# The last expert unit written apart, and the tail after it worked by halves of 512 features

## The chip, the cores and the metric

The kernel runs on one core of one Trainium2 chip. The metric is the device time of one launch in microseconds (us); lower is better. A core has five engines with instruction queues of their own: TensorE (PE; its weight loads are shown apart as PEld), VectorE (DVE), ScalarE (ACT), GpSimd (POOL) and SyncE (SP). They meet only through semaphores. All data here is fp32.

## The reference, cut to what matters

One inference step of a hybrid network of two layers for 128 context tokens (`x_prompt`) and 128 latent tokens (`x_sample`), 256 tokens of 1024 features. The last sub-layer of the second layer is a mixture of experts with a gated, normalised residual. With `x` the residual stream, `h` its normalised and modulated copy, and `g_mod` the gate of that sub-layer:

```python
logits = h @ w_router                      # (256, 8)
top_v, top_i = lax.top_k(logits, 2)
top_w = softmax(top_v)
gate = sum(one_hot(top_i, 8) * top_w[..., None], axis=1)
out = 0
for e in range(8):                         # D_FF_EXPERT = 2816
    out = out + gate[:, e:e+1] * ((silu(h @ wg[e]) * (h @ wu[e])) @ wd[e])
x = x + g_mod * rms_norm(out, gain)        # rms over the 1024 features
```

`x` is then returned as `y_prompt` and `y_sample`.

## The kernel before, in words

Everything up to the routing is the same in both kernels. What matters is the expert stage, from about 860 us to the end.

**Units.** Tokens are not sent to experts one by one. For each expert the kernel builds a selection matrix `SEL` (token by place, 86 places, `CAP`), so that one product with it gathers the expert's tokens. A unit is one expert with up to 86 of its tokens. Each expert has one unit; an expert with more tokens has further ones, at most 13 in all (`UNITS`). How many there are is known only on the chip: VectorE writes it into the table `TBL` (`unit_count`, L2846, in the first unit after its hidden block 12). With the inputs timed here there are 8 units, 0 to 7.

**A unit.** The hidden width 2816 is cut into 22 blocks of 128 (`HB`). For each block `t` TensorE makes gate and up products from the gathered tokens `XG` (`gate_up`, L1466), ScalarE takes the SiLU (L1971), VectorE multiplies (`mixed`, L2860), and TensorE multiplies the result with a slice of the down weights into banks 4 and 5 (`down`, L1486). `down(t - 1)` stands behind `gate_up(t)` in TensorE's queue, so that the other two engines have a gate and up product's time. The weights (1 MB and 512 KB for each block) come through a ring of 11 slots, issued by SyncE in the order of use; SyncE waits until TensorE has used the slot (`tile_used`, L543).

**Between units.** Ahead of the last `down` of a unit TensorE gathers the tokens of the next one (`gather`, L1432, with the selection that VectorE made in `next_selection`), and ScalarE copies them to `XG` (L1986). The output of a unit is features by places. VectorE copies it out of the banks (`copy_y`, L2853), TensorE turns it (`turn_y`, L1442), ScalarE copies it to `YG`, TensorE scatters it back to tokens with the transposed selection `SELT` (`scatter`, L1448), and VectorE adds it, times the routing weight `GT1`, to the sum `O` (L2904). All that is done within the first blocks of the next unit.

**Loops.** The unit's code stands three times on TensorE, ScalarE and VectorE: unit 0; a loop over units 1 to 6; a loop from unit 7 to the unit count, which each engine reads into a register from `TBL` (L1532 and L1533, L1992 and L1993, L2916 and L2923). The last unit therefore gathers as well, for a next one that isn't there. SyncE has the same loops for the weights.

**After the last unit.** The tail has nothing beside it. TensorE signals `units_done` (L1535), VectorE copies both halves, TensorE turns all eight blocks and, once ScalarE has both halves of `YG`, scatters (four products into banks 0 to 3). VectorE makes the four additions (L2931), then signals ScalarE with a small copy (L2933). ScalarE squares `O` for each of the two token groups (`norm_o`, L1572), loads the table with the square root, and takes the root (L1582). Meanwhile VectorE multiplies `O` with the modulation gate `GB` into `TO` (`gated`, L2046); then it takes the reciprocal (L2012) and writes `X` (`residual`, L2065). GpSimd waits for both halves of `X`, issues the two stores (L607, L608) and waits for them. L195 is the end of the program, where each engine drains and all meet.

Of the kernel before, what the change touches and what calls it, by code (L numbers as in the profile page):

```python
# [24 lines left out]
ALU = mybir.AluOpType  # L25
# [3 lines left out]
P = 128  # L29
D = 1024  # L30
# [162 lines left out]
def program(nc, t, out):  # L193
    ctx = ExitStack()
    with ctx:  # L195
# [226 lines left out]

        class Counts:
# [16 lines left out]
            @contextmanager  # L440
            def in_loop(self, i, n, per):

                self.base, self.n, self.per, self.i = self.n, {}, per, i
                yield
                got, self.n, self.i = self.n, dict(self.base), None
                assert got == per, got
                for name, k in got.items():
                    self.n[name] = self.base.get(name, 0) + n * k

# [16 lines left out]
        def _(sp):  # L466
# [85 lines left out]
            with sp.Fori(NE - 1, sp.value_load(TBL[0:1, UNITS:UNITS + 1], min_val=NE, max_val=UNITS)) as u:  # L552
                expert_tiles(u, sp.value_load(TBL[0:1, bass.ds(u, 1)], min_val=0, max_val=NE - 1))


        @block.gpsimd
        def _(pool):
# [54 lines left out]
            pool.wait_ge(sem("stored_y"), 32)  # L612
# [3 lines left out]
        def _(pe):  # L616
# [839 lines left out]
            def unit(u):  # L1456
# [22 lines left out]
                def down(t, arrived, due, hid):  # L1479
# [9 lines left out]
                    taken(ins)  # L1489
# [18 lines left out]
                if later:  # L1508
                    pe.wait_ge(sem("unit_taken"), u * 4 - 2)
# [31 lines left out]
            scatter(1, 2, "last_scattered")  # L1541
# [3 lines left out]
        def _(act):  # L1545
# [416 lines left out]
            def unit(u):  # L1962
# [11 lines left out]
                for h in range(0 if isinstance(u, int) else 2):  # L1974
                    act.wait_ge(sem("y_turned"), u * 2 + (h - 1))
                    A(YG[0:CAP, h * 512:(h + 1) * 512], bank[6 + h][0:CAP, :], ACT.Copy).then_inc(sem("unit_yg"), 1)
# [3 lines left out]
                with act.Fori(0, LOOPS) as i:  # L1980
                    for t in range(2, 2 + ROWS):
                        silu(t, u * UT + i * (3 * ROWS) + (N_MOE + gate_taken(t)), u * HB + i * ROWS + (FT + t - 1))
                taken(u * UT + (N_MOE + up_taken(HB - 1)))
# [6 lines left out]
            with act.Fori(1, NE - 1) as u:  # L1990
                unit(u)
            act.wait_ge(sem("table"), 1)  # L1992
            with act.Fori(NE - 1, act.value_load(TBL[0:1, UNITS:UNITS + 1], min_val=NE, max_val=UNITS)) as u:  # L1993
                unit(u)
# [8 lines left out]
        def _(dve):  # L2003
# [57 lines left out]
            def residual(n):  # L2061
                rstd()
                dve.wait_ge(sem("gated"), 2 * (n + 1))
                for st in range(NST):
                    v.scalar_tensor_tensor(X[:, st, :], TO[:, st, :], SM[:, 6 + st:7 + st], X[:, st, :],  # L2065
                                           ALU.mult, ALU.add).then_inc(sem("x_final" if n == 3 else "x"), 1)
# [779 lines left out]
            def unit_count():  # L2846
                v.tensor_scalar(TBLF[:, UNITS:UNITS + 1], ORDER[:, 2 * NE - 1:2 * NE], float(NE), None, ALU.add).then_inc(made("dve_chain"), 1)
                dve.wait_ge(sem("dve_chain"), so_far("dve_chain"))
                v.tensor_copy(TBL[:, :], TBLF).then_inc(made("table"), 1)
# [45 lines left out]
            def unit(u):  # L2895
# [5 lines left out]
                for st, h in ((0, 0), (0, 1), (1, 0), (1, 1)):  # L2901
                    dve.wait_ge(sem("scattered"), u * 4 + (2 * st + h - 3))
# [7 lines left out]
                next_selection(u)  # L2910
# [5 lines left out]
            units = dve.value_load(TBL[0:1, UNITS:UNITS + 1], min_val=NE, max_val=UNITS)  # L2916
            for name, k in per.items():
                counts.n[name] = counts.n.get(name, 0) - k
            n0 = dict(counts.n)
            with dve.Fori(1, NE - 1) as u, in_loop(u, NE - 1, per):  # L2920
                unit(u)
            counts.n = n0
            with dve.Fori(NE - 1, units) as u, in_loop(u, NE, per):  # L2923
                unit(u)
# [64 lines left out]
```

## Time and profile before

| | us |
|---|---|
| median of 3 runs | 1580.46 |
| lowest, highest | 1577.77, 1585.19 |
| the profiled execution, its own time | 1576.2 |
| its span in the trace | 1574.3 |
| TensorE busy, of the span | 1487.2 (94%) |
| VectorE busy | 545.6 (35%) |
| ScalarE busy | 296.3 (19%) |
| mean granted clock of TensorE | 0.984 |

The span runs from the first to the last instruction of the profiled execution. An engine is busy while one of its instructions runs; what it waits for is inferred from semaphores. The clock is a share of TensorE's full 2.4 GHz.

### The profile page before, as it was taken

To read this page: it belongs to the slowest core of one execution; us is meant where nothing else is said; L and a number is where in the kernel's file an instruction comes from. 1 tells how busy PE (TensorE), PEld (TensorE's weight loads), DVE (VectorE), ACT (ScalarE), POOL (GpSimd) and SP (SyncE) were. 2 spreads that over 40 slices of the span, in tenths; PEclk is the share of its full clock that TensorE was granted. 3 is DMA by queue.
4 is the path that set the end of the run, shared out by engine and by line. 5 is a ranking of instruction groups with operands and counts; after the bars stand their busy time and mean duration, and the time that the engine had idled before them with its cause. 6 is when DMAs were issued, how large, how long until landed. Compare 5 with 4: busy or idle time off the path is not lost.

```text
span 1574.3 us, 62507 instructions
## 1 busy us (share of the span) xinstructions
PE 1487.2 (94%) x28005; PEld 1323.4 (84%) x28005; DVE 545.6 (35%) x1410; ACT 296.3 (19%) x817; POOL 16.4 (1%) x32
## 2 busy tenths in 40 slices
PE   5999888999998999999887999999999999999995
PEld 3888477999546787888866999999999999999995
DVE  1463435666636344666843301010101011010102
ACT  2112423010102432444324101010101010010101
POOL 0100000000000000000000000000000000000000
PEclk9999998999998999999998999999999999999998
DMA  9722676444448144000132799999999999999993
GB/s 391 292 82 100 250 300 270 161 174 181 182 167 314 40 162 150 6 8 8 33 151 81 300 417 379 416 386 418 384 412 409 387 419 380 418 376 417 376 418 131
DMA packets 72895, 407.07 MB, mean 259 GB/s; under 512 B 10514, under 2 KB 10948, under 8 KB 35908
## 3 DMA queue, kind: packets, MB, share of 16 engines
q1 hardware_dynamic: 68176, 398.92, 64.0%
q0 software_dynamic: 1184, 3.41, 0.7%
q10 hardware_dynamic: 3412, 2.93, 0.6%
q8 instruction: 98, 1.61, 0.4%
q14 instruction: 25, 0.20, 0.0%
HBM read 403.31 MB, written 1.92 MB: 257 GB/s over the span
## 4 chain that ended last, share of the span: by engine, by line
PE 37%; PEld 10%; DVE 1%; ACT 1%; issue 1%; PEldq 0%; DVEq 0%; POOL 0%; ACTq 0%
PE bank L1466 20%; PE bank L1486 10%; PEld bank L1466 7%; PEld bank L1486 3%; PE bank L644 2%; PE bank L1448 1%; PE bank L1432 1%; PE bank L1442 0%; PEld bank L1432 0%; PE bank L709 0%; PE bank L1267 0%; PEld bank L1448 0%; DVE w L2036 0%; DVE w L2675 0%; PE bank L1290 0%
## 5 line engine op out<-in xcount | busy, mean ns | idle before, releaser
L1466 PE MATMUL bank<-w,ring 128*64 128x86 f32 x11264 | 452.6, 237 | 1.1 <-ACT w L1959 0.6
L1466 PEld LDWEIGHTS bank<-w,ring 128*64 128x64 f32 x11264 | 432.4, 136 | 9.7 <-issue 8.8
L1486 PE MATMUL bank<-w,ring 128*64 128x86 f32 x5632 | 238.7, 237 | 0.0
L2860 DVE TENSOR_TENSOR w<-w,bank 128x86 f32<-128x86 f32 x176 | 43.1, 245 | 549.0 <-PE bank L1466 541.6
L1486 PEld LDWEIGHTS bank<-w,ring 128*64 128x64 f32 x5632 | 220.8, 137 | 0.0
L1971 ACT ACTIVATE w<-bank 128x86 f32<-128x86 f32 x176 | 42.8, 243 | 572.4 <-PE bank L1466 572.4
L641 PE MATMUL bank<-w,ring 128*128 128x256 f32 x256 | 59.1, 394 | 4.3 <-DVE w L2454 3.7
L641 PEld LDWEIGHTS bank<-w,ring 128*128 128x128 f32 x256 | 50.5, 198 | 13.0 <-DVE w L2454 4.0
L644 PE MATMUL bank<-ring,w 128*128 128x256 f32 x256 | 56.0, 380 | 1.9 <-DVE w L2036 1.9
L644 PEld LDWEIGHTS bank<-ring,w 128*128 128x128 f32 x256 | 48.4, 190 | 8.8 <-DVE w L2036 2.3
L667 PE MATMUL bank<-ring,ct 128*32 128x256 f32 x768 | 47.0, 396 | 2.4 <-ACT ct L1569 2.1
L1201 PE MATMUL bank<-ht 64*64 64x64 f32 x1280 | 45.6, 219 | 2.4 <-issue 1.6
L970 PE MATMUL bank<-w 128*128 128x128 f32 x352 | 44.4, 281 | 1.3 <-DVE w L2352 1.3
L970 PE MATMUL bank<-ht,ring 128*128 128x128 f32 x352 | 44.7, 282 | 0.6 <-DVE ht L2028 0.6
L1201 PEld LDWEIGHTS bank<-ht 64*64 64x64 f32 x1280 | 42.2, 135 | 3.2 <-issue 1.9
L970 PEld LDWEIGHTS bank<-w 128*128 128x128 f32 x352 | 42.5, 198 | 1.5 <-DVE ring L2316 1.5
L745 PE MATMUL bank<-ht,ring 128*128 128x256 f32 x192 | 43.5, 383 | 0.0
L970 PEld LDWEIGHTS bank<-ht,ring 128*128 128x128 f32 x352 | 42.7, 198 | 1.0 <-issue 1.0
L970 PE MATMUL bank<-w,ring 128*128 128x128 f32 x352 | 42.9, 275 | 0.0
L667 PEld LDWEIGHTS bank<-ring,ct 128*32 128x32 f32 x768 | 23.9, 114 | 22.1 <-issue 4.5
L1003 PE MATMUL bank<-ring,w 128*128 128x512 f32 x88 | 42.2, 592 | 0.0
L748 PE MATMUL bank<-ring,ht 128*128 128x256 f32 (+1 forms) x192 | 42.0, 372 | 0.0
(437 smaller groups left out, 1795.9 us busy)
## 6 DMA issues: line engine op xcount, KB each, us to landing
ring<-in_moe_gu SPq DMA_DIRECT2D x176, 1024.0 KB, 8.5
ring<-in_moe_w_down SPq DMA_DIRECT2D x176, 512.0 KB, 8.6
ring<-in_ada_w SPq DMA_DIRECT2D x48, 1024.0 KB, 5.0
ring<-in_ev_w_in SPq DMA_DIRECT2D x11, 1024.0 KB, 26.6
ring<-in_ffn_w_gate SPq DMA_DIRECT2D x11, 1024.0 KB, 7.9
ring<-in_ffn_w_up SPq DMA_DIRECT2D x11, 1024.0 KB, 5.2
ring<-in_ffn_w_down SPq DMA_DIRECT2D x11, 1024.0 KB, 6.4
ring<-in_ev_w_out SPq DMA_DIRECT2D x4, 1024.0 KB, 11.0
```

The lines of the kernel that those rows point to most:

```text
L641: ins = mm(b[:, a * TW:(a + 1) * TW], w[:, k, a * P:(a + 1) * P], src[:, k, :], start=k == 0, stop=k == KC - 1)
L644: ins = mm(b[:, a * TW:a * TW + n], src[:, k, a * P:(a + 1) * P], w[:, k, 0:n], start=k == 0, stop=k == KC - 1)
L667: ins = mm(sums_bank(n)[32 * q:32 * q + 32, 0:TW], CT[:, NST * k:NST * k + 32], w[:, k % 2, q * TW:(q + 1) * TW], start=k == 0, stop=k == ...
L745: ins = mm(b[:, a * TW:(a + 1) * TW], w[:, k, a * P:(a + 1) * P], HT[:, k, :], start=k == 0, stop=k == KC - 1)
L748: ins = mm(b[:, a * TW:a * TW + n], HT[:, k, a * P:(a + 1) * P], w[:, k, 0:n], start=k == 0, stop=k == KC - 1)
L970: ins = mm(region(j, r)[:, which * P:(which + 1) * P], lhs(which, k), rhs(k), start=first and which == 0 and k == 0, stop=k == 3, skip_gro ...
L1003: ins = mm(bank[DOWN_BANK[p]][:, :], lhs, rhs, start=n == 0, stop=n == FT - 1)
L1201: ins = mm(z_bank(lv, 0)[hp, (4 * d + j) * DH:(4 * d + j + 1) * DH], IZ[hp, d, j, :], IP[i % 2][hp, d, j, :], start=True, stop=True)
L1466: ins = [mm(b[hp, 0:CAP], w[:, k, hp], XG[:, k, :], start=k == 0, stop=k == KC - 1, skip_group_check=True) for hp in HALVES]
L1486: ins = [mm(bank[4 + c // 4][hp, (c % 4) * CAP:(c % 4 + 1) * CAP], w[:, c * P + hp.start:c * P + hp.stop], HIDU[:, t % 2, :], start=t == 0 ...
L1971: A(SILU[:, t % 2, :], bank[t % 2][:, 0:CAP], ACT.Silu).then_inc(sem("silu"), 1)
L2860: v.tensor_tensor(HIDU[:, t % 2, :], SILU[:, t % 2, :], bank[2 + t % 2][:, 0:CAP], ALU.mult).then_inc(sem("hid"), 1)
```

## The change

- The loop over units 1 to 6 now runs to a last unit that is read from the table, and that last unit is written apart, with its number `last` and the one before it, `prev`, in registers. TensorE, ScalarE and VectorE read both values behind unit 0 (VectorE writes two more entries of the table). With 8 units the loop still runs over 1 to 6 and unit 7 stands apart. SyncE's loops stay.
- The last unit has no gather, no copies to `XG` and no next selection. Its last `down` signals each half of its output on its own.
- The tail goes by halves of 512 features, `h`, and by token groups, `st`. Each half is copied, turned and copied to `YG` on its own; the scatter begins with half 0 for both groups. The piece `n = 2 h + st` is added, squared, gated and given its residual by itself. ScalarE loads the table with the square root ahead of the tail (`load_root`). The mean square is made in two steps: VectorE scales the first halves' sums and adds epsilon, and the root takes the second halves' sums with that as its bias.
- The stores are issued by SyncE, four of 256 KB (128 rows of 2 KB), each as its piece of `X` is written. GpSimd has none and waits for none.

```diff
 # SyncE
+            for n in range(4):
+                h, st = divmod(n, 2)
+                sp.wait_ge(sem("x"), 6 + n + 1)
+                sp.dma_start(out[("y_prompt", "y_sample")[st]][0][:, h * 512:(h + 1) * 512],
+                             X[:, st, h * 512:(h + 1) * 512]).then_inc(sem("stored_y"), 16)
+            sp.wait_ge(sem("stored_y"), 64)
 # GpSimd
-            pool.wait_ge(sem("x_final"), 2)
-            pool.dma_start(out["y_prompt"][0], X[:, 0, :]).then_inc(sem("stored_y"), 16)
-            pool.dma_start(out["y_sample"][0], X[:, 1, :]).then_inc(sem("stored_y"), 16)
...
-            pool.wait_ge(sem("stored_y"), 32)
 # TensorE
-            def unit(u):
+            def unit(u, prev=None):
...
+                        if prev is not None and t == HB - 1 and c % 4 == 3:
+                            ins[0].then_inc(sem("last_down"), 1)
+                            ins[1].then_inc(sem("last_down"), 1)
+                    if prev is None or t < HB - 1:
+                        taken(ins)
...
-                pe.wait_ge(sem("sel"), u + 2)
                 pe.wait_ge(sem("selt"), u + 1)
-                gather()
+                if prev is None:
+                    pe.wait_ge(sem("sel"), u + 2)
+                    gather()
                 down(HB - 1, "slot_last", u * 16 + 16, u * HB + (FT + HB))
...
-            with pe.Fori(1, NE - 1) as u:
+            pe.wait_ge(sem("table"), 1)
+            last = pe.value_load(TBL[0:1, UNITS + 1:UNITS + 2], min_val=NE - 1, max_val=UNITS - 1)
+            prev = pe.value_load(TBL[0:1, UNITS + 2:UNITS + 3], min_val=NE - 2, max_val=UNITS - 2)
+            with pe.Fori(1, last) as u:
                 unit(u)
-            pe.wait_ge(sem("table"), 1)
-            units = pe.value_load(TBL[0:1, UNITS:UNITS + 1], min_val=NE, max_val=UNITS)
-            with pe.Fori(NE - 1, units) as u:
-                unit(u)
-            pe.drain().then_inc(sem("units_done"), 1)
-            pe.wait_ge(sem("last_y"), 2)
-            pe.wait_ge(sem("xg"), units * 2 + 2)
-            turn_y("last_turned")
-            pe.wait_ge(sem("last_y"), 4)
-            scatter(0, 0, "last_scattered")
-            scatter(1, 2, "last_scattered")
+            unit(last, prev)
+            for h in range(2):
+                pe.wait_ge(sem("last_y"), h + 1)
+                for c in range(4 * h, 4 * h + 4):
+                    ins = tr(bank[6 + h][0:CAP, (c % 4) * P:(c % 4 + 1) * P], YT[:, c, :], ident)
+                ins.then_inc(sem("last_turned"), 1)
+            for h in range(2):
+                pe.wait_ge(sem("last_yg"), h + 1)
+                for st in range(NST):
+                    mm(bank[2 * st + h][:, :], SELT[:, st, :], YG[0:CAP, h * 512:(h + 1) * 512],
+                       start=True, stop=True).then_inc(sem("last_scattered"), 1)
 # ScalarE (its loops as on TensorE; unit(last, prev) ends ahead of the copies to XG)
+            load_root()
             for h in range(2):
                 act.wait_ge(sem("last_turned"), h + 1)
-                A(YG[0:CAP, h * 512:(h + 1) * 512], bank[6 + h][0:CAP, :], ACT.Copy).then_inc(sem("last_y"), 1)
-            act.wait_ge(sem("o_ready"), 1)
-            norm_o()
+                A(YG[0:CAP, h * 512:(h + 1) * 512], bank[6 + h][0:CAP, :], ACT.Copy).then_inc(sem("last_yg"), 1)
+            for n in range(4):
+                h, st = divmod(n, 2)
+                act.wait_ge(sem("o_ready"), n + 1)
+                A(W[9][:, n * 512:(n + 1) * 512], O[:, st, h * 512:(h + 1) * 512], ACT.Square,
+                  accum_out=SQ4[:, n:n + 1]).then_inc(sem("out_squares"), 1)
+            act.wait_ge(sem("meansq"), 4)
+            act.wait_ge(sem("out_squares"), 16 + 4)
+            for st in range(NST):
+                ins = A(SM[:, 4 + st:5 + st], SQ4[:, 2 + st:3 + st], ACT.Sqrt, scale=1.0 / D, bias=SM[:, 2 + st:3 + st])
+            ins.then_inc(sem("root"), 1)
 # VectorE (its loops as on TensorE; unit(last, prev) has no next_selection)
-            dve.wait_ge(sem("units_done"), 1)
-            copy_y("last_y")
-            for st in range(NST):
-                for h in range(2):
-                    dve.wait_ge(sem("last_scattered"), 2 * st + h + 1)
-                    o = O[:, st, h * 512:(h + 1) * 512]
-                    v.scalar_tensor_tensor(o, bank[2 * st + h][:, :], GT1[:, st:st + 1], o, ALU.mult, ALU.add).then_inc(made("dve_chain"), 1)
-                    dve.wait_ge(sem("dve_chain"), so_far("dve_chain"))
-            v.tensor_copy(SM[:, 199:200], SM[:, 6:7]).then_inc(sem("o_ready"), 1)
-            gated(3)
-            residual(3)
+            for n in range(2):
+                dve.wait_ge(sem("last_down"), 2 * n + 2)
+                v.tensor_copy(YT[:, 4 * n:4 * n + 4, :].rearrange("p c n -> p (c n)"),
+                              bank[4 + n][:, 0:4 * CAP]).then_inc(sem("last_y"), 1)
...
+            for n in range(4):
+                h, st = divmod(n, 2)
+                dve.wait_ge(sem("last_scattered"), n + 1)
+                v.scalar_tensor_tensor(piece(O, n), bank[2 * st + h][:, :], GT1[:, st:st + 1], piece(O, n),
+                                       ALU.mult, ALU.add).then_inc(sem("o_ready"), 1)
+            dve.wait_ge(sem("gb_copied"), 16)
+            for n in range(2):
+                dve.wait_ge(sem("o_ready"), n + 1)
+                v.tensor_tensor(piece(TO, n), piece(O, n), piece(GB, n), ALU.mult).then_inc(sem("gated"), 1)
+            dve.wait_ge(sem("out_squares"), 16 + 2)
+            v.tensor_scalar(SM[:, 2:4], SQ4[:, 0:2], 1.0 / D, EPS, ALU.mult, ALU.add).then_inc(sem("meansq"), 1)
+            for n in range(2, 4):
+                dve.wait_ge(sem("o_ready"), n + 1)
+                v.tensor_tensor(piece(TO, n), piece(O, n), piece(GB, n), ALU.mult).then_inc(sem("gated"), 1)
+            rstd()
+            for n in range(4):
+                st = n % 2
+                dve.wait_ge(sem("gated"), 6 + n + 1)
+                v.scalar_tensor_tensor(piece(X, n), piece(TO, n), SM[:, 6 + st:7 + st], piece(X, n),
+                                       ALU.mult, ALU.add).then_inc(sem("x"), 1)
```

Waits inside a unit that were written with `u * k + c`, `c` negative, are written for the last unit with `prev` instead (`shifted_by`), to the same value.

## Rows read from the trace of the kernel before

**Rows 1.** Windows: us, busy by engine, clock, DMA share, GB/s

```profile
...
890.00:1550.00 660.00, 659.31 (x16808) 638.79 (x16806) 80.38 (x270) 57.68 (x204) 0.00 (x0) 1.00 0.98 398
...
```

**Rows 2.** Waits of SyncE's queue, 870 to 1576 us: total, times, longest

```profile
...
SPq L544 <- PE bank L1466: 383.3, 148, 19.5
...
```

**Rows 3.** Timeline of the tail: start, us, engine, line, instruction [idle before]

```profile
...
1548.62 0.24 DVE L2860 TENSOR_TENSOR w<-w,bank 128x86 f32<-128x86 f32 x1 [3.33 <-PE bank L1466]
1549.43 2.46 PEld L1432 LDWEIGHTS bank<-w 128*64 128x64 f32 x64
...
1551.89 1.35 PE L1486 MATMUL bank<-w,ring 128*64 128x86 f32 x32
...
1553.36 0.94 DVE L2853 COPY w<-bank 128x344 f32<-128x344 f32 x2 [4.49 <-PEq L1535]
...
1554.44 1.07 PE L1442 MATMUL bank<-cst,w 128*86 128x128 f32 x8 [1.20 <-DVE w L2853]
1555.11 1.08 ACT L1997 ACTIVATE w<-bank 86x512 f32<-86x512 f32 x2 [2.52 <-PE bank L1442]
...
1556.24 3.70 PE L1448 MATMUL bank<-w 86*128 86x512 f32 x8 [0.73 <-ACT w L1997]
...
1557.40 0.75 DVE L2931 SCALAR_TENSOR_TENSOR o<-bank,w,o 128x512 f32<-128x512 f32 x1 [3.10 <-PE bank L1448]
...
1558.33 2.47 DVE L2931 SCALAR_TENSOR_TENSOR o<-bank,w,o 128x512 f32<-128x512 f32 x3 [0.18 <-PE bank L1448]
...
1560.90 2.35 DVE L2046 TENSOR_TENSOR w<-o,gb 128x1024 f32<-128x1024 f32 x2
1561.02 1.06 ACT L1572 ACTIVATE w<-o 128x1024 f32<-128x1024 f32 x1 [4.83 <-DVE sm L2933]
...
1563.23 1.28 ACT L1582 ACT_TABLE_LOAD   x1
...
1564.85 0.17 DVE L2012 RECIPROCAL sm<-sm 128x2 f32<-128x2 f32 x1 [1.60 <-ACT sm L1582]
1565.05 2.48 DVE L2065 SCALAR_TENSOR_TENSOR x<-w,sm,x 128x1024 f32<-128x1024 f32 x2
1567.83 0.54 POOL L607 DMA_DIRECT2D out_y_prompt<-x  x1 [808.24 <-DVE x L2065]
1568.35 0.54 POOL L608 DMA_DIRECT2D out_y_sample<-x  x1
```

**Rows 4.** Groups by shape, 1549 to 1576 us: busy, mean ns of one

```profile
...
L2065 DVE SCALAR_TENSOR_TENSOR x<-w,sm,x 128x1024 f32<-128x1024 f32 x2 | 2.5, 1282 | 0.0
...
L2046 DVE TENSOR_TENSOR w<-o,gb 128x1024 f32<-128x1024 f32 x2 | 2.4, 1216 | 0.0
...
```

**Rows 5.** Line 195, each queue's end: duration min/median/max, first and last start

```profile
...
L195 SPq DRAIN  x1: 7/7/7, 1536.8 to 1536.8; - x1
...
L195 POOLq DRAIN  x1: 1693/1693/1693, 1572.4 to 1572.4; - x1
...
```

**Rows 6.** DMA issues, whole span: count, KB each, median us to landing

```profile
...
out_new_rwkv<-gb ACTq DMA_DIRECT2D x16, 32.0 KB, 2.1
...
out_y_prompt<-x POOLq DMA_DIRECT2D x1, 512.0 KB, 2.9
out_y_sample<-x POOLq DMA_DIRECT2D x1, 512.0 KB, 3.8
...
```

**Rows 7.** DMA issues, 845 to 858 us

```profile
...
ring<-in_moe_w_down SPq DMA_DIRECT2D x1, 512.0 KB, 3.6
```

**Rows 8.** Timeline of weight loads from unit 5 to unit 6

```profile
...
1379.32 1.26 PEld L1466 LDWEIGHTS bank<-w,ring 128*64 128x64 f32 x32
...
```

**Rows 9.** Timeline of weight loads from unit 6 to unit 7

```profile
...
1466.58 1.25 PEld L1466 LDWEIGHTS bank<-w,ring 128*64 128x64 f32 x32 [0.67 <-issue]
...
```

**Rows 10.** Line 1532, TensorE's queue

```profile
...
L1532 PEldq TENSOR_LOAD <-tbl x1: 485/485/485, 1465.4 to 1465.4; - x1
...
```

**Rows 11.** Timeline of weight loads, first gather

```profile
...
860.65 3.59 PEld L1432 LDWEIGHTS bank<-w 128*64 128x64 f32 x64 [0.97 <-DVE w L2788]
...
```

More of the change, by code:

```diff
@@ L420, in program, with shifted_by @@
         SELT = ROUTE[0:CAP, 768:1024].rearrange("p (s n) -> p s n", s=NST)
+        def shifted_by(u, prev, k, c):
+            return u * k + c if prev is None or c >= 0 else prev * k + (k + c)
         class Counts:
@@ L448, in in_loop, with in_last @@
                     self.n[name] = self.base.get(name, 0) + n * k
+            @contextmanager
+            def in_last(self, prev, n, per):
+                self.base = {name: self.n[name] - (n - 1) * k for name, k in per.items()}
+                self.n, self.per, self.i = {}, per, prev
+                yield
+                self.n, self.i, self.base = {}, None, {}
         class Walk:
@@ L1960, in _, with unit @@
                   ACT.Copy).then_inc(sem("xg"), 1)
-            def unit(u):
+            def unit(u, prev=None):
                 def taken(at):
@@ L1982, in unit @@
                         silu(t, u * UT + i * (3 * ROWS) + (N_MOE + gate_taken(t)), u * HB + i * ROWS + (FT + t - 1))
+                if prev is not None:
+                    return
                 taken(u * UT + (N_MOE + up_taken(HB - 1)))
@@ L1989, in _ @@
             unit(0)
-            with act.Fori(1, NE - 1) as u:
+            act.wait_ge(sem("table"), 1)
+            last = act.value_load(TBL[0:1, UNITS + 1:UNITS + 2], min_val=NE - 1, max_val=UNITS - 1)
+            prev = act.value_load(TBL[0:1, UNITS + 2:UNITS + 3], min_val=NE - 2, max_val=UNITS - 2)
+            with act.Fori(1, last) as u:
                 unit(u)
-            act.wait_ge(sem("table"), 1)
-            with act.Fori(NE - 1, act.value_load(TBL[0:1, UNITS:UNITS + 1], min_val=NE, max_val=UNITS)) as u:
-                unit(u)
+            unit(last, prev)
+            load_root()
             for h in range(2):
                 act.wait_ge(sem("last_turned"), h + 1)
-                A(YG[0:CAP, h * 512:(h + 1) * 512], bank[6 + h][0:CAP, :], ACT.Copy).then_inc(sem("last_y"), 1)
-            act.wait_ge(sem("o_ready"), 1)
-            norm_o()
+                A(YG[0:CAP, h * 512:(h + 1) * 512], bank[6 + h][0:CAP, :], ACT.Copy).then_inc(sem("last_yg"), 1)
[9 more added lines that the diff above has]
+            ins.then_inc(sem("root"), 1)
         @block.vector
@@ L2893, in first_unit, with unit @@
                         unit_count()
-            def unit(u):
+            def unit(u, prev=None):
                 dve.wait_ge(sem("tile_used0"), u * UT + N_MOE)
@@ L2909, in unit @@
                 mixed(1, u * HB + (FT + 2), u * UT + (N_MOE + up_taken(1)))
-                next_selection(u)
+                if prev is None:
+                    next_selection(u)
                 for t in range(2, HB):
@@ L2915, in _ @@
             first_unit()
-            units = dve.value_load(TBL[0:1, UNITS:UNITS + 1], min_val=NE, max_val=UNITS)
+            last = dve.value_load(TBL[0:1, UNITS + 1:UNITS + 2], min_val=NE - 1, max_val=UNITS - 1)
+            prev = dve.value_load(TBL[0:1, UNITS + 2:UNITS + 3], min_val=NE - 2, max_val=UNITS - 2)
             for name, k in per.items():
                 counts.n[name] = counts.n.get(name, 0) - k
-            n0 = dict(counts.n)
-            with dve.Fori(1, NE - 1) as u, in_loop(u, NE - 1, per):
+            with dve.Fori(1, last) as u, in_loop(u, NE - 1, per):
@@ L2933, in _, with piece @@
-            v.tensor_copy(SM[:, 199:200], SM[:, 6:7]).then_inc(sem("o_ready"), 1)
-            gated(3)
-            residual(3)
+            with counts.in_last(prev, NE - 1, per):
+                unit(last, prev)
+            for n in range(2):
+                dve.wait_ge(sem("last_down"), 2 * n + 2)
+                v.tensor_copy(YT[:, 4 * n:4 * n + 4, :].rearrange("p c n -> p (c n)"),
+                              bank[4 + n][:, 0:4 * CAP]).then_inc(sem("last_y"), 1)
+            def piece(b, n):
+                h, st = divmod(n, 2)
+                return b[:, st, h * 512:(h + 1) * 512]
@@ new lines, in _ @@
+            for n in range(4):
+                h, st = divmod(n, 2)
+                dve.wait_ge(sem("last_scattered"), n + 1)
+                v.scalar_tensor_tensor(piece(O, n), bank[2 * st + h][:, :], GT1[:, st:st + 1], piece(O, n),
+                                       ALU.mult, ALU.add).then_inc(sem("o_ready"), 1)
+            dve.wait_ge(sem("gb_copied"), 16)
+            for n in range(2):
+                dve.wait_ge(sem("o_ready"), n + 1)
+                v.tensor_tensor(piece(TO, n), piece(O, n), piece(GB, n), ALU.mult).then_inc(sem("gated"), 1)
```

15 lines of the change are left out of this document (7 added, 8 removed).

## The prediction

> **What bounds the kernel now.** I read the granted clock and the expert stretch first. From 890 to 1550 us TensorE is busy 659.31 of 660.00 us at a granted clock of 1.00 (the 2.4 GHz level), while the DMA engines are busy 0.98 of the time [rows 1]. The waits of SyncE's queue say which of the two waits: SyncE stood 383.3 us behind TensorE's products for a free slot [rows 2], so the weights run ahead and TensorE sets the end of every expert unit. Then I read the tail from the timeline and the chain of waits. After the last product of the last unit nothing overlaps any more: each operation waits for the one before it, so each microsecond removed there is a microsecond of the total. The reader should see in [rows 3] one staircase: gather (1549.43), the last down product (1551.89 to 1553.24), copy, turn, copy, scatter (1556.24), four additions (to 1560.80), gating and squares side by side (1560.90, 1561.02), a table load (1563.23), the residual (to 1567.53), two stores from GpSimd's queue (1567.83). After the last landing GpSimd's queue drains for 1.693 us [rows 5], and only then the span ends at 1574.3. I cost the change against this execution (span 1574.3, own time 1576.2, so 1.9 us lie around the span), and carry the difference over to the median 1580.46, which is 4.3 us above it. The runs shown differ by 7.4 us; a difference under 0.5% (7.9 us) is about what a measurement of this kernel cannot tell from no change.
>
> **1. The gather of the last unit goes.** It holds TensorE from 1549.43 until the down product's start, 1551.89 - 1549.50 = 2.4 us [rows 3] (the first product follows the first weight load by 0.07). Its cover goes with it: the down product now follows the one before directly and needs VectorE's last hidden block. That ended at 1548.62 + 0.24 = 1548.86 [rows 3], 0.6 us before the gather began, so no new wait. The last 512 KB of weights were issued long before and SyncE waits for TensorE, not the reverse [rows 2]. **Gain 2.4 us.** The selection that VectorE no longer makes, and the copies to XG on ScalarE, were beside TensorE's work: nothing.
>
> **2. Copy, turn and scatter by halves.** Let 0 be the start of the last down product. Before, the copies start at 1.47 and both end at 2.41, the turn starts at 2.55, ScalarE's copy at 3.22, the scatter at 4.35 [rows 3]. After, the first copy lies under the second half of the down product. The second starts at 1.47 and lasts half of 0.94; its four transposes start at 2.1 and leave TensorE at 2.6. The first half was turned behind the down product, from 1.4, and 0.67 later (the distance from the turn to ScalarE's copy) ScalarE starts its half of 0.54 to 0.59 us: ready at 2.7. The scatter starts at 2.7 rather than 4.35. **Gain 1.65 us** (at least 1.0, if the first half stands behind the second in TensorE's order; at most 1.9). Scatter to last addition is the same 3.8 plus 0.75 us, paced by TensorE's four products; the order of the halves changes no count. The last addition ends at 7.3, formerly 8.9.
>
> **3. Gate, squares, root, residual.** Before, from the last addition (1560.80) to the last of X (1567.53) there are 6.73 us [rows 3]: VectorE's gates are hidden by squares, table load and root on ScalarE. Now the table load (1.28) is issued behind the last SiLU, where ScalarE has nothing until the first turned half: hidden; uncovered it would cost its 1.28. Squares of 512 take no more than the 1.06 of one of 1024; each can follow its addition, so three of four are hidden under the additions and the last under the gates. VectorE becomes the bound. The pace of its long operations in a row is 2.35 / 4 = 0.59 us for a gated half and 2.48 / 4 = 0.62 for a residual half [rows 3], if a half costs half. A lone operation takes longer than the pace of two (1.216 and 1.282 us mean against 1.18 and 1.24 in a row) [rows 4], so I take 0.60 and 0.67. Sum: two gates 1.2, mean square 0.17 (like the reciprocal, 1564.85), two gates 1.2 (over the root), reciprocal 0.2, four residuals 2.65: 5.4 us. **Gain 1.3 us** (0.5 if each half pays another 0.1; 1.6 if a half costs half). The Trainium skill, page "VectorE: DVE Perf Modes", section "The TRN2 errata", speaks against this part: operations on SBUF pay a fixed cost per instruction, and its formula for fp32 tensor_tensor, (N+151)/0.96 ns, gives 1.224 us at N=1024, which the trace bears out (1.216), and 0.69 at 512; by it, as an estimate, the eight halves cost 0.7 us more than I take, a gain of 0.6.
>
> **4. The register loads move.** TensorE reads the unit count once now, between units 6 and 7, where the weight loads pause: 0.67 us idle [rows 9], against none noted from unit 5 to 6 [rows 8]. After, it reads two values, between units 0 and 1, and none later. One TENSOR_LOAD is 0.485 us [rows 10]; with its checks a second costs about 0.85 if they run in series. **Loss 0.85 us** (0 if the second hides under the first, 1.5 at most). ScalarE and VectorE make theirs where they otherwise wait 3 us for TensorE. The table is written after block 12 of 22 in unit 0, so the earlier wait for it is free. Nothing is queued on DMA behind it.
>
> **5. The stores.** Before, 1567.53 to the landing of the second half MB at 1568.35 + 3.8 = 1572.15 are 4.6 us [rows 3, 6]: 0.8 until its issue, then 3.8. After, SyncE issues four of 256 KB, the first three while VectorE still works; nothing else is in its queue by then. A 32 KB store from ScalarE's queue landed 2.1 us after issue, the first 512 KB store 2.9 [rows 6], a lone 512 KB load on SyncE's queue 3.6 [rows 7]. These bound a last 256 KB between 2.1 and 3.6; I take 2.6, near the first rows because they are stores. **Gain 2.0 us** (1.0 to 2.5). The Trainium skill, page "DMA: Bandwidth & Descriptors", section "Anatomy of one DMA", has 2.0 us plus bytes over 436 GB/s: 2.6 for 256 KB, an estimate; for 512 KB it would say 3.2, where the trace has 2.9 and 3.8.
>
> **6. The end.** The last landing (1572.15) to the span's end (1574.3) is 2.15 us, of which GpSimd's drain is 1.693 [rows 5]. GpSimd stood idle for 808 us before its stores [rows 3]; it has no wait left there now and can drain in that time. SyncE's own drain took 0.007 us. About 0.35 us of handshakes stays. **Gain 1.8 us** (0 if GpSimd's drain is no work of its own but comes with the end; 1.9 at most).
>
> **Sum.** 2.4 + 1.65 + 1.3 - 0.85 + 2.0 + 1.8 = 8.3 us: span 1566.0, own time 1567.9, and 1580.46 - 8.3 = 1572.2 us on the scale of the median.
>
> **Rivals.**
> A, all six as above: 1572.2, own range 1570.5 to 1574.0. Chance 0.62.
> B, the end does not shorten: the drain stays about 1.7 us whoever waits last, or the four small stores land no sooner than GpSimd's two. For it: neither is shown on SyncE's queue in the tail. Against it: its drain of 0.007 us [rows 5]. Gain 8.3 - 1.8 = 6.5 or 8.3 - 2.0 = 6.3, so 1574.1. Chance 0.19.
> C, the halves give nothing: fixed costs of twice as many instructions and semaphores take what parts 2 and 3 give. The skill's rule above points this way, but only by 0.7 of the 2.95. Gain 2.4 - 0.85 + 2.0 + 1.8 = 5.35: 1575.1. Chance 0.14.
> D, slower: the pause of TensorE between units 0 and 1 grows to about 1.5 us, and the granted clock falls to its lower level, 1.2 GHz. When the first gather ran partly at that level, its 64 weight loads took 3.59 us [rows 11] against 2.46 later [rows 3], 46% more. The gain of 8.3 is eaten after 18 us at the low level, and 35 us of it give 1580.2 + 7.9 = 1588. Against it: the clock held 1.00 through the idle 0.67 us between units 6 and 7. Chance 0.03; 0.02 is for what I don't see.
>
> **How the numbers follow.** The likeliest is A, 1572.2. The range takes in A to C and about 2 to 3 us for where a median of such runs falls: 1568.5 to 1577.5. The threshold of 7.9 us lies just under A's 8.3, with terms uncertain by about 1 us together: somewhat over half of A passes it, and with noise a few of B and C. Faster 0.44, same 0.52, slower 0.04.
>
> **What would show it.** Right: no gather before the last down product, the scatter's start 2.7 us behind that product's start; the last table load under the last unit; VectorE busy without a gap over 0.3 us from the additions to X; last X 12.6 to 12.8 us behind the down product's start; the last store landing 2.6 us later; the span's end within 0.5 us of it; 1.4 to 1.6 us idle weight loads between units 0 and 1. Wrong: a long drain on SyncE or GpSimd after the landing, stores queued behind each other past 3.5 us, a second table load on a copy or square, a fall of the granted clock after 945 us, or a wait for the last hidden block.

## The result and the profile after

The changed kernel takes 1569.06 us in the median of 7 runs (1566.97 to 1573.01), the kernel before 1579.59 us (1574.78 to 1585.19). The ratio is 0.9937, with a 95% interval of 0.9923 to 0.9951: 10.0 us faster by the ratio, 7.7 to 12.2. The forecast was 8.3 us and 1572.2. The ratio itself lies beyond 0.9950, so "faster by over 0.5%", to which I gave 0.44, is the likelier case; its interval reaches 0.9951, so it is not shown beyond noise that the gain passes 0.5%. That there is a gain is shown.

The profiled execution has a span of 1570.8 us, only 3.5 less than before. That is no measure of the change: its first gather began 5.4 us later than in the trace of before, in stages that are the same in both. So I take distances inside the expert stage, from the same kind of instruction to the same kind.

The tail, from the timeline of the changed kernel (start, us, engine, line, instruction, idle time before it):

```profile
...
1554.48 2.44 PEld L1501 LDWEIGHTS bank<-w,ring 128*64 128x64 f32 x64
1554.55 2.54 PE L1501 MATMUL bank<-w,ring 128*64 128x86 f32 x64
1554.86 0.24 DVE L2899 TENSOR_TENSOR w<-w,bank 128x86 f32<-128x86 f32 x1 [3.33 <-PE bank L1481]
...
1556.57 1.11 DVE L2966 COPY w<-bank 128x344 f32<-128x344 f32 x2 [1.47 <-PE bank L1501]
...
1557.15 1.23 PE L1558 MATMUL bank<-cst,w 128*86 128x128 f32 x8
...
1557.82 1.19 ACT L2024 ACTIVATE w<-bank 86x512 f32<-86x512 f32 x2 [2.33 <-PE bank L1558]
...
1558.47 3.70 PE L1563 MATMUL bank<-w 86*128 86x512 f32 x8
...
1559.63 3.33 DVE L2977 SCALAR_TENSOR_TENSOR o<-bank,w,o 128x512 f32<-128x512 f32 x4 [1.95 <-PE bank L1563]
...
1560.42 0.63 ACT L2028 ACTIVATE w<-o 128x512 f32<-128x512 f32 x1 [1.41 <-DVE o L2977]
...
1562.87 1.28 DVE L2982 TENSOR_TENSOR w<-o,gb 128x512 f32<-128x512 f32 x2
1562.99 0.63 ACT L2028 ACTIVATE w<-o 128x512 f32<-128x512 f32 x1
...
1564.07 0.16 DVE L2984 TENSOR_SCALAR sm<-sm 128x2 f32<-128x2 f32 x1
1564.14 1.29 DVE L2987 TENSOR_TENSOR w<-o,gb 128x512 f32<-128x512 f32 x2
1564.27 0.48 ACT L2033 ACTIVATE sm<-sm 128x1 f32<-128x1 f32 x2 [0.56 <-DVE sm L2984]
1565.35 0.16 DVE L2047 RECIPROCAL sm<-sm 128x2 f32<-128x2 f32 x1
1565.54 2.74 DVE L2992 SCALAR_TENSOR_TENSOR x<-w,sm,x 128x512 f32<-128x512 f32 x4
...
1568.31 0.33 SPq L570 DMA_DIRECT2D out_y_sample<-x  x1
```

Its first two rows hold the last two down products, 64 pairs; the second begins after 32 of them, at 1554.55 + 1.19 = 1555.74. There is no gather between them (before: 1549.43 to 1551.89 [rows 3]). VectorE's last hidden block ended at 1555.10, 0.6 us ahead of the product that needs it. Counted from 1555.74, the start of the last down product, the scatter starts 2.73 later (4.35 before), the last addition ends 7.22 later (8.91), the last of X is written at 1568.28, 12.54 later (15.64). VectorE goes from its last addition to the last of X with no gap over 0.05 us. ScalarE's squares keep one addition behind it, and its root (1564.27) is over before the gates are.

The stores on SyncE, KB each and us from issue to landing:

```profile
...
out_y_prompt<-x SPq DMA_DIRECT2D x2, 256.0 KB, 2.1
out_y_sample<-x SPq DMA_DIRECT2D x2, 256.0 KB, 2.1
```

The last is issued at 1568.31 and lands 2.1 us later, 1570.4. At the end of the program (line 195: duration, first and last start):

```profile
...
L195 POOLq DRAIN  x1: 1534/1534/1534, 819.0 to 819.0; - x1
...
L195 SPq DRAIN  x1: 7/7/7, 1570.6 to 1570.6; - x1
...
```

GpSimd's drain of 1.534 us is still there, but it runs at 819 us. From the last write of X to the end of the span there are 2.53 us, before 1574.30 - 1567.53 = 6.77.

The weight loads at the boundary of units 0 and 1, and of units 6 and 7, in the changed kernel:

```profile
...
951.37 1.26 PEld L1501 LDWEIGHTS bank<-w,ring 128*64 128x64 f32 x32
953.71 1.25 PEld L1481 LDWEIGHTS bank<-w,ring 128*64 128x64 f32 x32 [1.08 <-issue]
...
```

```profile
...
1471.54 1.25 PEld L1501 LDWEIGHTS bank<-w,ring 128*64 128x64 f32 x32
1472.72 1.26 PEld L1481 LDWEIGHTS bank<-w,ring 128*64 128x64 f32 x32
...
```

From the last down product to the next gate product it is 2.34 us at the first boundary and 1.18 at the second. In the kernel before, the down product and the next gate product at the first boundary, and the down product at the second:

```profile
...
945.56 1.27 PEld L1486 LDWEIGHTS bank<-w,ring 128*64 128x64 f32 x32
946.74 1.28 PEld L1466 LDWEIGHTS bank<-w,ring 128*64 128x64 f32 x32
...
```

```profile
...
1464.65 1.25 PEld L1486 LDWEIGHTS bank<-w,ring 128*64 128x64 f32 x32
...
```

So it was 1.18 us at the first, and 1466.58 - 1464.65 = 1.93 at the second [rows 9]: 1.16 us lost at one, 0.75 won at the other. The two register loads of the changed kernel (line, queue, duration in ns, start):

```profile
...
L1550 PEldq TENSOR_LOAD <-tbl x1: 481/481/481, 951.9 to 951.9; - x1
...
```

```profile
...
L1551 PEldq TENSOR_LOAD <-tbl x1: 306/306/306, 952.8 to 952.8; - x1
...
```

### The profile page after: what moved, and what is told of

Its sections match the earlier page's. It is cut to its first block, busy times and chain, and to the rows that moved or that the text cites. A ratio compares the mean times of both kernels' runs of the same rounds, so it can differ in the third digit from the quotient of the medians.

```text
span 1570.8 us, 62378 instructions
## 1 busy us (share of the span) xinstructions
PE 1487.5 (95%) x27941; PEld 1323.2 (84%) x27941; DVE 545.6 (35%) x1413; ACT 296.6 (19%) x821; POOL 15.3 (1%) x30
## 4 chain that ended last, share of the span: by engine, by line
PE 48%; DVE 1%; ACT 1%; issue 0%; DVEq 0%
PE bank L1481 27%; PE bank L1501 13%; PE bank L659 2%; PE bank L1463 2%; PE bank L1447 1%; PE bank L1457 0%; PE bank L1563 0%; PE bank L724 0%; PE bank L1282 0%; PE bank L1534 0%; DVE w L2071 0%; DVE w L2710 0%; PE bank L1305 0%; PE bank L1417 0%; ACT o L1595 0%
```

## The experiments

The unit of comparison is the same in all: from the start of the last down product to the last write of X ("to X"), and from there to the end of the span ("X to end"). Before they are 15.64 and 6.77 us, in the changed kernel 12.54 and 2.53. A part that an edit doesn't touch came out within 0.04 us of these in every trace, so differences of some tenths of a us can be read, which the whole time cannot show. E5 to E8 have one run each, so only the distances of their traces are read.

**E1. The stores back on GpSimd.**

```diff
 # SyncE: the four stores and their wait go; GpSimd:
+            pool.wait_ge(sem("x"), 10)
+            pool.dma_start(out["y_prompt"][0], X[:, 0, :]).then_inc(sem("stored_y"), 16)
+            pool.dma_start(out["y_sample"][0], X[:, 1, :]).then_inc(sem("stored_y"), 16)
...
+            pool.wait_ge(sem("stored_y"), 32)
```

> The changed kernel with its stores put back on GpSimd: two of 512 KB, once all four pieces of X are written. Measure: from the last write of X to the end of the span, 2.5 us in the changed kernel, 6.8 before. If the queue and the place of GpSimd's drain make the gain of the stores (my theory): 6.5 to 6.9 again, with a drain of 1.5 to 1.7 us behind the last landing, and a ratio to the kernel before of 0.9937 + 4.2/1580 = 0.9964. If the rest of the change is what shortened the end (rival): it stays under 4 us, ratio near 0.994.

X to end 6.78 us, to X 12.58. The drain stands behind the landing again:

```profile
...
L195 POOLq DRAIN  x1: 1693/1693/1693, 1569.8 to 1569.8; - x1
...
```

Ratio to the kernel before 0.9979 (0.9963 to 0.9995), which holds the 0.9964 expected, at its edge. All of the 4.24 us comes back with GpSimd's two stores; the rest of the change has no part in it.

**E2. Two stores of 512 KB on SyncE.**

```diff
-            for n in range(4):
...
+            sp.wait_ge(sem("x"), 9)
+            sp.dma_start(out["y_prompt"][0], X[:, 0, :]).then_inc(sem("stored_y"), 16)
+            sp.wait_ge(sem("x"), 10)
+            sp.dma_start(out["y_sample"][0], X[:, 1, :]).then_inc(sem("stored_y"), 16)
```

> The changed kernel with two stores of 512 KB on SyncE, each when its token group of X is written, in place of four of 256 KB. If the gain lies in the queue alone (rival): the span still ends 2.5 us behind the last write of X. If the halves matter because the data flow starts earlier (my theory): 1 MB at the 400 GB/s of the trace takes 2.6 us and starts two pieces, 1.3 us, later, so 3.3 to 3.9 us.

X to end 3.73 us, against 2.53 with four stores; ratio 0.9932 (0.9906 to 0.9958). By the trace four pieces earn 1.2 us over two; the whole time, with its wider interval, does not show it. The landings of the two stores:

```profile
...
out_y_prompt<-x SPq DMA_DIRECT2D x1, 512.0 KB, 2.7
out_y_sample<-x SPq DMA_DIRECT2D x1, 512.0 KB, 3.3
```

The second waits behind the first's data: 3.3 us rather than 2.7.

**E3. The tail of the kernel before, behind a last unit without gather.**

```diff
 # SyncE: two stores as in E2 (waits on x 7 and 8)
 # TensorE
+            pe.wait_ge(sem("last_y"), 2)
+            turn_y("last_turned")
+            pe.wait_ge(sem("last_yg"), 2)
+            scatter(0, 0, "last_scattered")
+            scatter(1, 2, "last_scattered")
 # ScalarE
-            load_root()
...
+            act.wait_ge(sem("o_ready"), 5)
+            norm_o()
 # VectorE: copies, additions by token group, the small copy, then
+            gated(3)
+            residual(3)
```

> The changed kernel with the last unit apart and without gather, but the tail of the kernel before: whole copies, turn, scatter by token group, squares and gates of 1024, the table load behind the squares; two stores of 512 KB on SyncE. Measure: from the start of the last down product to the last write of X, 12.54 us in the changed kernel, 15.64 before. If the halves earn the 3.1 us (my theory): 15.4 to 15.7. If they give nothing and the missing gather alone moved the tail (rival C): under 13. Ratio to the kernel before by mine 0.9937 + (3.1 + 1.2)/1580 = 0.9964.

To X 15.55 us, X to end 3.18; ratio 0.9967 (0.9946 to 0.9989). Gates, table load and residual stand as before:

```profile
...
1559.20 2.35 DVE L2066 TENSOR_TENSOR w<-o,gb 128x1024 f32<-128x1024 f32 x2
...
1561.52 1.28 ACT L1599 ACT_TABLE_LOAD   x1
...
1563.35 2.48 DVE L2085 SCALAR_TENSOR_TENSOR x<-w,sm,x 128x1024 f32<-128x1024 f32 x2
...
```

The tail by halves earns 15.55 - 12.54 = 3.0 us, with all that belongs to it: the squares by pieces, the mean square in two steps and the early table load. The missing gather has no part in it. Rival C falls.

**E4. The kernel before, only its stores on SyncE.**

```diff
 # GpSimd: both stores and its wait for them go; SyncE:
+            sp.wait_ge(sem("x_final"), 1)
+            sp.dma_start(out["y_prompt"][0], X[:, 0, :]).then_inc(sem("stored_y"), 16)
+            sp.wait_ge(sem("x_final"), 2)
+            sp.dma_start(out["y_sample"][0], X[:, 1, :]).then_inc(sem("stored_y"), 16)
+            sp.wait_ge(sem("stored_y"), 32)
```

> The kernel before with nothing changed but the stores: two of 512 KB, issued by SyncE, each when its token group of X is written; GpSimd stores and waits for nothing there. From the last write of X to the end of the span, 6.8 us before. If the queue and the drain are separate from the rest of the change (my theory): 3.3 to 3.9 us, so 2.9 to 3.5 faster, ratio near 0.998. If the drain moves to whoever waits last: 5 us or more.

X to end 3.17 us, 3.6 less; to X 15.66, unchanged. The ratio, 0.9987 (0.9969 to 1.0006), holds 3.6 us (0.9977) and zero. The drains:

```profile
...
L195 POOLq DRAIN  x1: 1534/1534/1534, 813.6 to 813.6; - x1
...
L195 SPq DRAIN  x1: 7/7/7, 1574.0 to 1574.0; - x1
...
```

SyncE waits last and drains in 0.007 us; GpSimd's 1.534 us have gone to 813.6 us. This edit also lets the first store go out as soon as its token group is written, which the kernel before does not; so the 3.6 us are of queue and start together, and it is the rows of the drains that part them. Rival B falls with E1 and E4.

**E5. TensorE's register loads inside unit 0.**

```diff
                 pe.wait_ge(sem("selt"), u + 1)
+                if not later:
+                    pe.wait_ge(sem("table"), 1)
+                    read["last"] = pe.value_load(TBL[0:1, UNITS + 1:UNITS + 2], ...)
                 if prev is None:
                     pe.wait_ge(sem("sel"), u + 2)
                     gather()
+                if not later:
+                    read["prev"] = pe.value_load(TBL[0:1, UNITS + 2:UNITS + 3], ...)
                 down(HB - 1, ...)
```

> The changed kernel with TensorE's two register loads moved into unit 0: one ahead of its gather, one ahead of its last down product, where matmuls still stand in TensorE's queue. In the changed kernel the start of unit 1's first gate product is 2.34 us behind the start of unit 0's last down product, against 1.18 us from one unit to the next elsewhere. If the idle time is the queue running dry during two loads in series (my theory): the two are hidden or nearly, 1.2 to 1.5 us. If a load costs its 0.5 us wherever it stands (rival): the same 1.1 us of idle time, now in two places.

The last down product but one, the gather, the last down product and the next unit's first gate product, as weight loads:

```profile
...
943.68 1.27 PEld L1501 LDWEIGHTS bank<-w,ring 128*64 128x64 f32 x32
945.40 2.45 PEld L1447 LDWEIGHTS bank<-w 128*64 128x64 f32 x64 [0.45 <-issue]
947.87 1.26 PEld L1501 LDWEIGHTS bank<-w,ring 128*64 128x64 f32 x32
949.03 1.07 PEld L1481 LDWEIGHTS bank<-w,ring 128*64 128x64 f32 x26
```

The distance that I had named is 1.21 us, as if all were hidden. But the first load now costs ahead of the gather: 945.40 - 943.68 = 1.72 us, with 0.45 idle, where 1.19 is usual, and the gather itself takes 2.47 in place of 2.39. Over the three together the loads cost 949.03 - 943.68 - 4.76 = 0.6 us, against 1.16 in the changed kernel. So half my theory: one load is hidden, the other is not. The hidden one:

```profile
...
L1550 PEldq TENSOR_LOAD <-tbl x1: 308/308/308, 947.1 to 947.1; - x1
...
```

It starts at 947.1, when the gather's weight loads still run for 0.7 us (to 947.85), and with its checks it stops the queue for no longer than that. The other starts at 944.6 (line 1545, 0.485 us), only 0.4 us ahead of the end of the down product's (944.95), and stops the queue for 0.86: what is left is the 0.45 idle. That it starts so late because a loop's branch and the wait for the table stand in front of it is likely and not shown. The distance named before the run does not show this loss.

**E6. No table load ahead of the tail.**

```diff
-            load_root()
             for h in range(2):
                 act.wait_ge(sem("last_turned"), h + 1)
```

> The changed kernel without the early load of the table with the square root, which is then loaded at the root itself. If the 1.28 us are only partly exposed, because VectorE's gates 2 and 3 run beside it (my theory): the load starts when the mean square is there, the root ends 1.8 us behind it, 0.7 to 0.8 us after the gates, and the last write of X is 0.7 to 0.8 us later (13.3 us behind the start of the last down product, from 12.54). If the table is free anyway or squares had hidden it: no difference. If the whole load is exposed: 1.3 us.

To X 12.83 us: 0.29 later, not 0.7. ScalarE's rows say why:

```profile
...
1562.47 0.19 ACT L2027 ACTIVATION_READ_ACCUMULATOR w<-o 128x1 f32 x1
1562.73 1.28 ACT L2032 ACT_TABLE_LOAD   x1
1564.03 0.48 ACT L2032 ACTIVATE sm<-sm 128x1 f32<-128x1 f32 x2
```

The table load did not wait for the mean square. It started at 1562.73, 0.07 after the last square's accumulator was read and 0.3 before VectorE began the mean square, and only its last part was exposed: VectorE stood idle for 0.17 us ahead of the reciprocal. The program has two waits in front of the root. The one for the squares is an instruction of its own in the trace, and the load stands behind it:

```profile
...
L2030 ACTq EVENT_SEMAPHORE  x1: 17/17/17, 1562.7 to 1562.7; - x1
...
```

The one for the mean square (line 2029) has no instruction of its own; it is carried by the root's instruction, and holds the root alone, not the load. Of 1.28 us the early load saves 0.29, which is part of the 3.0 us of E3.

**E7. Two gates on GpSimd.**

```diff
 # GpSimd
+            pool.wait_ge(sem("gb_copied"), 16)
+            for st in range(NST):
+                pool.wait_ge(sem("o_ready"), st + 1)
+                g.tensor_tensor(TO[:, st, 0:512], O[:, st, 0:512], GB[:, st, 0:512], ALU.mult).then_inc(made("pool_chain"), 1)
 # VectorE: gates 0 and 1 go; residuals 0 and 1 wait for pool_chain 5 and 6
```

> The changed kernel with the gating products of pieces 0 and 1 on GpSimd, beside the additions of pieces 2 and 3. If VectorE is the bound from the last addition to X (my theory): the last write of X comes about 1.0 us earlier, 11.5 us behind the last down product's start, less what GpSimd takes of VectorE's access to memory. If the root through ScalarE bounds it (rival): at most 0.4 us, with VectorE idle ahead of the reciprocal.

To X 11.55 us, 1.0 less. VectorE's, GpSimd's and ScalarE's rows:

```profile
...
1557.88 3.33 DVE L2981 SCALAR_TENSOR_TENSOR o<-bank,w,o 128x512 f32<-128x512 f32 x4 [1.95 <-PE bank L1567]
...
1558.80 2.49 POOL L631 TENSOR_TENSOR w<-o,gb 128x512 f32<-128x512 f32 x2 [795.86 <-DVE o L2981]
...
1561.12 0.20 DVE L2985 TENSOR_SCALAR sm<-sm 128x2 f32<-128x2 f32 x1
1561.24 1.28 DVE L2988 TENSOR_TENSOR w<-o,gb 128x512 f32<-128x512 f32 x2
...
1562.05 0.48 ACT L2037 ACTIVATE sm<-sm 128x1 f32<-128x1 f32 x2
1562.56 0.17 DVE L2051 RECIPROCAL sm<-sm 128x2 f32<-128x2 f32 x1
1562.76 2.74 DVE L2996 SCALAR_TENSOR_TENSOR x<-w,sm,x 128x512 f32<-128x512 f32 x4
...
```

GpSimd takes 1.25 us for a gate that takes VectorE 0.68, but beside it. The additions still take 3.33 us and the gates 1.28. VectorE has no idle time ahead of the reciprocal, so in the changed kernel it bounded this stretch. Here the root ends at 1562.53 and the gates at 1562.52: the two are level, and taking more work off VectorE ahead of the reciprocal would gain nothing. The drain grows, and still ends before the stores do:

```profile
...
L195 POOLq DRAIN  x1: 3322/3322/3322, 1559.5 to 1559.5; - x1
...
```

**E8. The gather of the last unit kept.**

```diff
                 if prev is None:
                     pe.wait_ge(sem("sel"), u + 2)
-                    gather()
+                gather()
```

> The changed kernel with the gather of the last unit kept (its result is not used). If the gather stands alone on TensorE's path (my theory): the span's tail from unit 7's last hidden block is 2.4 us longer and the part behind the last down product is unchanged at 15.06 us. If its absence exposed a wait for the last hidden block (rival): the difference is under 2.4, and the changed kernel shows idle weight loads ahead of the last down product.

VectorE's last hidden block and the last down product:

```profile
...
1550.88 0.24 DVE L2899 TENSOR_TENSOR w<-w,bank 128x86 f32<-128x86 f32 x1 [3.33 <-PE bank L1481]
...
1554.12 1.42 PE L1501 MATMUL bank<-w,ring 128*64 128x86 f32 x32
...
```

From the start of the one to the start of the other it is 3.24 us, against 0.87 in the changed kernel and 3.26 before; the part behind is 12.56 + 2.54 us, unchanged. The gather is worth 2.37 us, and nothing else waits for its absence.

**E9 and E10. Loads and gates together, beside the changed kernel again.** E9 is the edits of E5 and E7 in one; E10 is the changed kernel unaltered.

> The changed kernel with both: TensorE's two register loads inside unit 0, and the gating products of pieces 0 and 1 on GpSimd. If the two places are independent, as each stands on the only chain there is at its time (my theory): the start of unit 1 gains 1.1 us, the last write of X 1.0 us, the span 2.1 us against the changed kernel, so near 0.9937 - 0.0013 = 0.9924 of the kernel before. If the chip's clock or the runs' spread takes it (rival): no difference that the intervals can part, but the two distances in the trace stay.

> The changed kernel unaltered, beside e9 on the same chip and against the same runs of the kernel before. The distances in its trace add up to 9.3 us: gather 2.4, halves 3.1, stores and end 4.2, register loads -0.4. If that sum is the whole gain (my theory): ratio 0.9941, with an interval that holds it, and from the first gather to the end 8.9 to 9.3 us less than before. If there is something more in the earlier stages (rival, since the first median was 10.5 us lower): ratio below 0.993, and the first gather starts earlier than before.

E9: 1568.89 us, ratio 0.9928 (0.9906 to 0.9951); to X 11.56 and X to end 2.54, the register loads as in E5. E10: 1571.01 us, ratio 0.9937 (0.9916 to 0.9958); to X 12.54, X to end 2.55. E9 has kept both distances, 1.0 and 0.6 us, but the difference of the ratios, 1.4 us, lies inside their intervals: E9 is shorter by the trace and not shown faster by the timed runs. E10 repeats 0.9937, and the 9.3 us of the trace (0.9941) lie inside both intervals.

Is there a gain in the earlier stages? The first gather of E10 began at 864.7 us, in the kernel before at 860.65, and in the ten other traces between 859.4 and 866.1. The stages ahead vary from execution to execution by more than any term of the sum, so no gain of some tenths could be seen there, and nothing speaks for one.

From the first gather to the end E10 took 706.07 us, 7.6 less than before, outside the 8.9 to 9.3 that I had expected (the first trace of the changed kernel has 8.9). The 1.7 us missing from the 9.3 stand in two places. Unit 0, from the first gather to the next, took 0.45 us more than before. And from the gather behind unit 0 to the one behind unit 1 it was 88.82 us, where the first trace of the changed kernel has 87.58. Most of that is a pause in the middle of a gate product of unit 1, for which the profile names no wait:

```profile
...
976.46 1.69 PEld L1481 LDWEIGHTS bank<-w,ring 128*64 128x64 f32 x43 [0.97 <-issue]
...
```

Such pauses stand in other traces as well: 0.4 to 0.8 us in unit 7 in E3, E4, E6, E7 and E9, so also with the code of the kernel before (E4), and 2.4 us in unit 0 of E2. They stand where TensorE goes through a copy of the unit's code for the first time, which would fit a wait for code; no run tests that, and the sum of distances leaves them out. Without pauses and register loads a unit takes 86.5 us in both kernels, counted from gather to gather.

## Why the prediction was right

The direction, the mechanism and the range held; the gain in the trace is 2.39 + 3.10 - 0.41 + 4.24 = 9.3 us, where I had 8.3. The measured median, 1569.06, is 3.1 us under the forecast of 1572.2 and only 0.6 above the range's lower end: 1.0 us is the error of the terms, 0.9 is that the kernel before has a median of 1579.59 in seven runs where I started from 1580.46 in three, and 1.2 is left to the spread of the runs.

- **Gather.** 2.4 us forecast, 2.39 in the trace and 2.37 in E8. Its cover was not needed: 0.6 us of margin, as reckoned.
- **Copy, turn, scatter.** Scatter at 2.73 us, forecast 2.7; last addition at 7.22, forecast 7.3.
- **Gate to X.** 12.54 - 7.22 = 5.3 us, forecast 5.4. Halves cost about a tenth more than a half: two gates 1.28 us, four residuals 2.74, forecast 1.2 and 2.65. The fixed cost of the Trainium skill's page "VectorE: DVE Perf Modes", section "The TRN2 errata", is borne out for the duration of one operation (0.68 us in E1, 0.69 by its formula) and not as a price in a row, where the second gate adds 0.60 (1.28 for two): by it I would have sized the gain at 0.6 us, where the trace shows 6.73 - 5.32 = 1.4. E3 shows 3.0 us for both steps together, forecast 2.95.
- **What was right in result and wrong in reason.** I gave the early table load a price of 1.28 us if uncovered. E6 shows 0.29, since the load passes ahead of the wait for the mean square.
- **Register loads.** The mechanism was right, the size too large: forecast a net loss of 0.85 us, measured 0.41. Two things were off. I priced the second load like the first, 0.85 us with its checks, and it stopped the queue for 0.65. And I took the part of the first that is hidden to be the same in both places. It is not: the old load started 0.5 us before TensorE's weight loads ran out (1465.4, against 1464.65 + 1.25), the new one 0.7 before (951.9, against 951.37 + 1.26). These two make the 0.4 us between forecast and trace. The 0.65 is no saving by nearness: in E5, with the whole gather between the two, the second load is as short.
- **Stores.** The term most off: forecast a gain of 2.0 us, measured 4.6 - 2.1 = 2.5. I took 2.6 us for a last store of 256 KB with others ahead of it; it landed in 2.1. The data went at about 395 GB/s, so a piece takes 0.66 us, which is the distance between the issues: none stood behind another. A store of 512 KB with hardly any data ahead of it on this queue landed in 2.7 (E2's first, both of E3 and E4), 0.6 more for 256 KB more; by the two, as an estimate, some 1.5 us do not hang on the size. That my row of a 32 KB store has 2.1 as well [rows 6] is then no support for the number. The page "DMA: Bandwidth & Descriptors" of the Trainium skill, section "Anatomy of one DMA", gives 2.6 for 256 KB, but its fit is for GpSimd's queue; on SyncE's the trace has 2.1. The two stores in the order of the kernel before (E3, E4) end 0.6 us later than the four; two stores behind the new order of halves, 1.2 later (E2).
- **The end.** 1.8 us forecast; 2.15 before and about 0.4 after are 1.75. E1 and E4 turn it on and off with the queue that stores: from the last landing to the end there are 2.2 us with GpSimd and 0.4 with SyncE.
- **The chances.** The threshold sat 0.4 us below A's forecast. The two terms that I missed most, stores and register loads, both err to the side of a larger gain; that they did not cancel is luck, and without it the gain would have lain near the threshold. I held "same" (0.52) for likelier than what came. Rival D stayed away: the granted clock is 1.00 in every window from 900 to 1550 us of the changed kernel, through 1.08 us of idle weight loads. (The price that I gave to D is not sound: its 46% is of a gather that ran only partly at the lower level, and its sum starts from 1580.2 where the median was 1580.46.)
- **The signs.** Three of those that I named lay a little off: the last of X at 12.54 us (12.6 to 12.8), the last landing after 2.1 (2.6), 1.08 us of idle weight loads (1.4 to 1.6). The others came as named, and none of the signs of being wrong did.

What stays open is only the size of the whole: the ratios give 10.0 us with 2.2 to either side, the trace 9.3, and the runs cannot tell these apart.

## What to carry to other kernels

In a tail where one operation waits for the next, reckon from a fixed point inside the last busy stage, distance by distance; the spans of two executions differ by more than the change is worth. Look at the drains at the program's end: the last wait belongs on a queue whose drain is short, and work on GpSimd belongs early enough that its drain is over. When an instruction is moved out of a loop's end, measure over everything between two unchanged neighbours, since the cost can have moved by one step. And ask how far the queue runs ahead of the engine at the new place: that much of the instruction is free.

## What the runs showed of the hardware

- GpSimd's drain at the program's end took 1.53 us with nothing queued for long before it (E4, and the changed kernel), 1.69 behind its own stores (E1), and 3.32 when issued with its last product running, 1.5 to 1.6 us past that product's end (E7). SyncE's took 0.007.
- The second register load of TensorE took 0.306 us in the changed kernel, 0.330 in E10 and 0.308 in E5, where the first took 0.481 to 0.485. In E5 the whole gather stands between the two, so it is not that the second follows at once; the reason is open. With its checks the second stopped TensorE's queue for 0.65 us in the changed kernel, the first for 0.86.
- In E6 the table load started 0.07 us after ScalarE's last operation, behind the program's wait for the squares and 0.3 us before VectorE began the mean square, which the root's own instruction waits for.
- Four stores of 256 KB, 0.66 us apart on SyncE's queue, each landed in 2.1 us; two of 512 KB, as close, in 2.7 and 3.3; the two on GpSimd's queue in 3.0 and 3.8:

```profile
...
out_y_prompt<-x POOLq DMA_DIRECT2D x1, 512.0 KB, 3.0
out_y_sample<-x POOLq DMA_DIRECT2D x1, 512.0 KB, 3.8
```
